# Moving the SBUF layout of a two-block transformer kernel down by 128 and 160 bytes

## The reference, cut to what matters

```
q = (h @ wq)                                # 8 heads, 2 x 128
s = einsum('nhpd,hpkd->nhpk', q, keys)      # 2 x 128 keys a head
top 16 of each half -> 256 candidates -> best 16 of 16384 experts
act = gelu(einsum('nd,nhkd->nhk', h, u_tab[idx]))
y   = einsum('nhk,nhkd->nd', gate * act, v_tab[idx])
```

## Time and profile before

| | before |
|---|---|
| median of 3 runs | 2292.7 us |
| the three runs | 2286.57, 2292.7, 2293.03 us |
| the profiled execution: its time | 2286.57 us |
| its span, first to last instruction | 2285.2 us |
| PE busy | 2234.8 us (98%) |
| DVE busy | 1867.5 us (82%) |
| ACT busy | 1199.8 us (53%) |
| mean granted PE clock | 0.993 |
| DMA | 442.32 MB, mean 194 GB/s |

### The profile page before, as it was taken

One profiled execution on the slowest core, in us unless ns is written; L12 is line 12 of the kernel. 1 busy time (PEld: TensorE's weight loads), 2 busy tenths in 40 slices (PEclk: granted clock), 3 DMA queues, 4 the chain that ended last, 5 costly groups with the idle time before them and its releaser, 6 DMA issues.

```text
span 2285.2 us, 34776 instructions
## 1 busy us (share of the span) xinstructions
PE 2234.8 (98%) x13446; PEld 1886.9 (83%) x13446; DVE 1867.5 (82%) x3365; ACT 1199.8 (53%) x1754; POOL 168.7 (7%) x75
## 2 busy tenths in 40 slices
PE   9999999999999999999999999999999999999997
PEld 7789978777888888888887877788888888887886
DVE  8679996568688988888888888869998888887656
ACT  7555554466456565554444545455665554444553
POOL 0000000000044400000000000024430000000000
PEclk9999999999999999999999999999999999999999
DMA  8366593233555555555558996456655555556674
GB/s 292 125 206 219 193 357 114 92 120 99 187 175 185 185 176 174 175 168 175 174 175 306 338 360 230 148 184 187 187 184 171 175 171 172 176 175 219 219 238 136
DMA packets 123508, 442.32 MB, mean 194 GB/s; under 512 B 13760, under 2 KB 16832, under 8 KB 122704
## 3 DMA queue, kind: packets, MB, share of 16 engines
q1 hardware_dynamic: 117464, 425.04, 56.5%
q10 hardware_dynamic: 5880, 15.06, 2.0%
HBM read 436.88 MB, written 3.16 MB: 193 GB/s over the span
## 4 chain that ended last, share of the span: by engine, by line
PE 83%; DVE 9%; ACT 3%; DMA 2%; issue 2%; SPq 0%; ACTq 0%; DVEq 0%
PE psum L442 21%; PE psum L450 14%; PE psum L452 13%; PE psum L451 13%; PE psum L443 10%; PE psum L445 3%; PE psum L2864 3%; DVE low L2600 2%; PE psum L444 1%; DVE acc L1777 1%; DVE cv L2108 1%; DMA ring<-in_peer_v 1%; PE psum L918 1%; ACT cv L1398 1%; ACT spl L1097 1%
## 5 line engine op out<-in xcount | busy, mean ns | idle before, releaser
L2600 DVE TENSOR_TENSOR low<-ring,spl 128x1024 fp32r<-128x1024 f32 x638 | 778.8, 1228 | 258.1 <-ACT spl L1097 257.1
L1097 ACT ACTIVATE spl<-ring 128x1024 fp32r<-128x1024 f32 x702 | 735.2, 1053 | 283.3 <-DMA ring<-in_peer_u 160.5
L442 PE MATMUL psum<-hT,spl 128*128 128x512 f32 x2016 | 728.3, 400 | 1.8 <-DVE hT L1757 1.8
L443 PE MATMUL psum<-hT,low 128*128 128x256 f32 x2016 | 565.5, 281 | 0.0
L442 PEld LDWEIGHTS psum<-hT,spl 128*128 128x128 f32 x2016 | 380.7, 189 | 79.6 <-issue 2.6
L450 PE MATMUL psum<-spl,Ws 128*128 128x512 f32 x1024 | 406.9, 397 | 7.0 <-DVE Ws L2638 7.0
L452 PE MATMUL psum<-spl,Ws 128*128 128x512 f32 x1024 | 399.5, 390 | 0.0
L451 PE MATMUL psum<-low,Ws 128*128 128x512 f32 x1024 | 398.3, 389 | 0.0
L443 PEld LDWEIGHTS psum<-hT,low 128*128 128x128 f32 x2016 | 382.4, 190 | 9.8
L1706 ACT ACTIVATE Ws<-S 128x256 fp32r<-128x256 f32 x256 | 106.7, 417 | 357.9 <-PE psum L452 353.1
L2921 POOL TENSOR_TENSOR low<-ring,spl 128x1024 fp32r<-128x1024 f32 x64 | 162.3, 2537 | 1134.8 <-ACT spl L1097 1134.8
(11 more groups left out here) (413 smaller groups left out, 3039.5 us busy)
## 6 DMA issues: line engine op xcount, KB each, us to landing
ring<-in_peer_u SPq DMA_DIRECT2D x256, 512.0 KB, 3.5
ring<-in_peer_v SPq DMA_DIRECT2D x256, 512.0 KB, 3.6
vring<-in_ada_w SPq DMA_DIRECT2D x56, 512.0 KB, 5.8
ring<-in_w_up SPq DMA_DIRECT2D x44, 512.0 KB, 5.1
aring<-in_ada_w SPq DMA_DIRECT2D x40, 512.0 KB, 5.0
ring<-in_ab_in SPq DMA_DIRECT2D x32, 512.0 KB, 3.5
ring<-in_peer_wq SPq DMA_DIRECT2D x32, 512.0 KB, 4.3
ring<-in_w_down SPq DMA_DIRECT2D x22, 512.0 KB, 5.4
```

Of the source, the lines that this page charges most:

```text
L442: q.matmul(b[:, :].rearrange("p (z t) -> p z t", z=2), l[0], r, start=start, stop=False)
L443: return q.matmul(b[:, 0:256], l[1], r[:, 0], start=False, stop=False)
L1097: q.activation(P.spl[:, m % SLOTS, 0:w], P.ring[:, m % SLOTS, 0:w], ACT.Copy).then_inc(*P.hi.mark(m))
L2600: q.tensor_tensor(P.low[:, n % SLOTS, 0:w], P.ring[:, n % SLOTS, 0:w], P.spl[:, n % SLOTS, 0:w].bitcast(F32), ALU.subtract).then_inc(*P.lo ...
```

## The change

Three numbers of the layout change. `base` goes from 16640 to 16512, `eps1` gets 8 columns in place of 16, and `cT` goes from word 33968 to 33960 of the arena. Every fixed tensor from `ring` to `eps1` starts 128 bytes lower. The arena starts 160 bytes lower, at byte 82,528, and every tensor in it moves by that, `cT` by 192.

The ring's slots and the slots of `spl` then start 128 bytes past a multiple of 256 (they stay at multiples of 64). The arena starts 32 bytes past a multiple of 64 and 96 past one of 256. So the arena tensors at multiples of 64 bytes (xr, aring, vring, acc, aT, cR, MT, Ws, S, keys, qT, mR and the rest) go to 32 bytes past one, the twelve named above go to multiples of 64, and `cT` is at a multiple of 64 before and after. No instruction, wait, size of an operation or queue order changes. The waits of the program keep every overlap that existed apart, and `cT` takes the eight words behind `mv` that nothing used.

```diff
-        self.base = 16640
+        self.base = 16512
...
-        self.eps1 = f("eps1", [128, 16])
+        self.eps1 = f("eps1", [128, 8])
...
-        self.cT = a("cT", 33968, [128, 2, 3, 256], F32R)
+        self.cT = a("cT", 33960, [128, 2, 3, 256], F32R)
```

## The result

The changed kernel takes 2307.76 us (median of 4 runs, 2306.46 to 2309.11), the kernel before 2292.12 us (4 runs, 2286.57 to 2293.03). The ratio is 1.008, with a 95% interval of 1.0067 to 1.0093; it is that of the means of all runs on record, 2309.3 us over 15 runs of the changed kernel to 2291.0 us over the 4, while the two medians alone stand at 1.0068. The profiled executions differ by more than the medians, 2310.5 against 2285.2 us of span, 25.3 us: the one before is the fastest of its runs, and the one after is near the top of its 15.

A forecast was written before the change was run, and what follows sets the result against it. PE, busy 98% of the span, was taken to bound the kernel. Four terms of 0 summed to 0 against the profiled 2286.57 us; the forecast was the runs' median, 2292.7 us, range 2285 to 2302.

The forecast's parts named there:

- `cT` and `eps1` cost 0: Early first stage: `cT` rows are written and read once, `eps1` loses unused columns; both cost 0.
- PE operands: PE loads and products on moved operands: at most +2 ns a load, hidden, and +1 ns a moving operand; taken as 0.
- the 32 ns of the prediction: v part: a matmul starts each 0.22 us and a `Ws` load takes 188 ns, leaving 32 ns of cover.
- DVE and ACT operands: DVE and ACT work on arena tensors: at most 0.5% on DVE, ACT no dearer; cost 0, upper bound some 1 us.
- DMA writes: Ring and ada tiles written to SBUF rows off 256-byte boundaries: cost 0, upper bound 1.2%, read from `rmask` and `pm`.
- The first rival: DMA tile rows each cost one 256-byte piece more, +6.2%, showing where engines are full: 2296 to 2302 us; chance 0.12.
- The second rival: DVE or PE pays for arena operands off 64 bytes; 35 ns more a `Ws` load would give 2302 us; chance 0.04.
- it gets faster: Twelve tensors moved to multiples of 64, or the fixed-to-arena distance, save over 0.3%, some 2284 us; chance 0.05.
- The signs of being right: `Ws` loads 188 ns, `low` 1229 ns, u and v windows 57.1 busy us, queue near 56.5%, PE waits within 2 us.
- 0.84 for the same: Whole kernel: chance 0.84 of staying within 0.3%, against 0.11 for slower and 0.05 for faster.
- bounds of +1 and +2 ns: PE: upper bounds of +1 ns for a product's moving operand and +2 ns for a weight load.
- The forecast of the base: Time taken for the kernel before: 2292.7 us, from three runs of 2286.57, 2292.7 and 2293.03.

The follow-up runs named there:

- the base run: Kernel before with only `base` lowered from 16640 to 16512, all tensors down by 128 bytes, the distances kept: 2291.38 us, ratio 1.0013.
- the run with 32/96/160: Kernel before with its three `Ws` buffers 32, 96 and 160 bytes past where they were, `Eb` moved up behind them: ratio 1.0078.
- the table: Product times from three runs of the kernel before, `Ws` buffers moved 0/64/128, 32/96/160 and 0/192/224 bytes: ratios 1.0058, 1.0078, 1.0026.
- the run with ring and `spl` moved: Kernel before with ring, `low` and `spl` down by 128 bytes, `hT` and arena where they were: 2308.66 us, ratio 1.0091.
- the ring at 64: Kernel before with ring and `low` 192 bytes lower (64 more, modulo 256), all else where it was: 2304.31 us, ratio 1.0077.

## Why the prediction was wrong, by its steps

- *No added instruction or wait; `cT` and `eps1` cost 0.* Right as far as it goes: the counts are equal and the base run, with `hT`, ring and arena moved together, is 0.13% slower.
- *PE operands: "all of it is hidden; ... I take 0."* This is the step that failed: a term taken as 0 that measured 16.6 us in the v parts. It priced each operand by its own place. By that measure nothing changed: the load of `Ws` is 188 ns before and after, and `mkT` at 380 ns in the earlier trace rows is 380 ns after, though it went to a multiple of 64. The cost sits in the pair. The load runs while the product before it streams, and at the wrong distance the pitch of the products grows by 6.6 ns, although the load alone would fit under them with 226.7 - 188 = 39 ns to spare (the 32 ns of the prediction come from a start read to 10 ns). The rows chosen did hold pairs at other distances: `mkT` and its stationary `mqT` are 160 bytes past a multiple of 256 apart, `pm` and `pp` a multiple, and they take 380 and 379 ns; the second block of `P5` in the earlier trace rows is 128 bytes off against `ident`, and these transposes take 272 ns by the median both there and in the changed kernel, where the two blocks are 224 and 96 bytes off. So the effect does not show in those plain float32 products of 128 and 256 columns, and what the rows lacked was a product of 512 columns in the rounded format with its pair at another distance.
- *DVE and ACT operands: 0.* Right. The product with `rmask` takes 555 ns at its new place (556 in its median before), DVE's busy time rose by 1.5 us in 1867.5, and the loss went with three PE operands put back.
- *DMA writes: 0 with an upper bound of 1.2%.* Nothing speaks against the 0, though the runs cannot measure 1.2%. The ring's queue fell from 56.5% to 54.1%, the fullest windows have the same share as the earlier trace rows, and they move 378 to 411 GB/s against 394 to 419; the run with 32/96/160, whose ring rows lie at multiples of 256, moves 382 to 406 there.
- *The first rival, one more 256-byte piece a row* (0.12), named the likeliest way to be slower and asked for 60% in the queue; it did not come. The doubt that the prediction raised itself, of full engines, is answered by the base run as well.
- *The second rival, DVE or PE pays for arena operands off 64 bytes* (0.04), had the place and the sign, with the wrong rule and the wrong meter. It wanted a load above 220 ns; the load never moved. It ruled itself out by a threshold that belongs to a load waiting for its turn, and the cost was in the product beside it. As a rule it is refuted by 64 and 128 bytes in the table and by the run with ring and `spl` moved.
- *The rival "it gets faster"* (0.05) named the cause in half a sentence, "something in the distance between fixed tensors and arena (32 bytes less) matters, of which no row tells", with the wrong sign and no price. It was not followed up.
- *The signs of being right* nearly all came: loads at 188 ns, `low` at 1228 ns, full u and v windows, no more waiting. They watched waits and loads, and a slower product hides in a window that is busy anyway; the count of products in the window or their pitch was the sign that was missing.
- *The range, 2285 to 2302, and 0.84 for the same.* Too narrow and too sure. The price per product was 2.9% of its pitch, on products that are most of the v parts; bounds of +1 and +2 ns taken from plain float32 products and from loads were no bound for the stream.
- *The forecast of the base* was the median of three runs that lay high; over 25 runs the kernel before stands at 2287.5 us. This does not change the verdict.

The Trainium skill (SBUF — State Buffer, "Who interferes with whom") gives PE two independent read ports, one for the moving operand and one for the weights, and says that PE never waits on anyone. The traces do not speak against it for the other engines: after the change the pitch is 233.2 ns with DVE, ACT and POOL idle and 233.4 ns with DVE at work. They differ for PE's own two reads: the same product takes 389 ns or up to 398 ns by the distance between them. The measurement decides.

What stays open is the mechanism. A clash of PE's two reads in some structure of SBUF that repeats after 256 bytes would fit the runs in which one distance changes, but no run shows such a structure, nor which of the two reads is held up. Why 64 and 192 differ, why the ring at 64 costs as much as it does, and why products of 256 columns with `hT` are fastest at 192 of the distances tried, is not explained. Of the 25.3 us between the two profiled executions, 16.6 are in the v parts and about 2.6 are the products with `aT` and `cR`; of the other 6 us, the 3.2 in the u parts lie within what these parts vary by with no operand of theirs moved (up to 4.4 us), and the rest was not pinned down.

## What to carry to other kernels

When PE is the bound and streams wide products back to back, the SBUF addresses of the moving and of the stationary operand are a tuning knob. For products of 512 columns in the rounded 32-bit format with the weights' slots as moving operand, keep their distance at a multiple of 256 bytes, and change a layout only in steps that keep it. For other shapes measure first: the products of 256 columns above were 4% faster at 192. A few bytes saved in a small tensor ahead of an arena can cost 1% of the kernel. And judge such a change by the pitch, start to start over some thirty products: neither the loads nor any wait showed it, and the products' durations, whose ends are modelled, showed 5 to 6 ns of the 6.6.

## What the runs showed of the hardware that was not expected

- The distance modulo 256 bytes between the operand that streams and the one that is loaded at the same time changes a 128x512 product's pitch, in the rounded 32-bit format, from 226.7 to 233.3 ns; 0 is the cheapest of the eight distances in steps of 32 bytes, 96 the dearest (389 to 397 or 398 ns for two of its three products).
- For products of 256 columns with `hT` moving over weights from `spl`, 0 is not the cheapest: their pitch is 119.7 ns there and 114.6 ns at 192.
- The absolute place does not matter at this scale: all tensors 128 bytes lower gave 1.0013, ring and `spl` 256 bytes lower 1.0009.
- Rows written 128 bytes past a 256-byte boundary do not cost the 6.2% that one more piece a row would be: the ring's queue holds 54.1% of the engines' time after the change and 55.9% in the base run, against 56.5% before.
